# Hybrid decoder layer, one core: the FFN's second weight product by seven block products instead of eight

## The reference

```python
x = layer_norm(ALPHA * x + mix @ w_out, ln1_g, ln1_b)
gate, up = jnp.split(x @ w_ffn_in, 2, axis=-1)             # w_ffn_in: 1024 x 5632
x = layer_norm(ALPHA * x + (jax.nn.silu(gate) * up) @ w_ffn_out, ln2_g, ln2_b)   # w_ffn_out: 2816 x 1024
```

## Time and profile before

| | before |
|---|---|
| time, 3 runs | 2395.21, 2398.1 (median), 2398.82 us |
| span of the profiled execution, first to last instruction | 2396.9 us |
| TensorE busy in it | 2353.9 us (98%) |
| GpSimd, VectorE, ScalarE busy | 1246.0, 1317.3, 1003.4 us |
| mean clock granted to TensorE | 0.993 |
| mean DMA rate | 144 GB/s |
| products of pair 1 and 2 | from about 1266 and 1820 us |
| halves of pair 1 and 2 | from about 1617 and 2173 us |

### The profile page before, as it was taken

One profiled execution on the slowest core, in us unless ns is written; L12 is line 12 of the kernel. 1 busy time (PEld: TensorE's weight loads), 2 busy tenths in 40 slices (PEclk: granted clock), 3 DMA queues, 4 the chain that ended last, 5 costly groups with the idle time before them and its releaser, 6 DMA issues.

```text
span 2396.9 us, 33703 instructions
## 1 busy us (share of the span) xinstructions
PE 2353.9 (98%) x12883; PEld 2259.9 (94%) x12883; DVE 1317.3 (55%) x2034; ACT 1003.4 (42%) x1678; POOL 1246.0 (52%) x679
## 2 busy tenths in 40 slices
PE   8899999999999999999999999999999999999997
PEld 7899999999999989999999999999999999999997
DVE  4455564554666564576365765554064675554165
ACT  4335554554555533355343444333243444333243
POOL 4455545544454445455455555555465555555543
PEclk9999999999999999999999999999999999999999
DMA  6444534434366765554543223226543222226453
GB/s 213 135 113 134 152 98 136 121 102 135 110 181 197 230 220 174 207 198 171 213 153 115 81 77 105 82 87 222 196 159 133 82 77 98 89 76 236 158 190 109
DMA packets 147492, 345.31 MB, mean 144 GB/s; under 512 B 14366, under 2 KB 93302, under 8 KB 145142
## 3 DMA queue, kind: packets, MB, share of 16 engines
q1 hardware_dynamic: 147334, 343.17, 44.3%
HBM read 290.30 MB, written 53.84 MB: 144 GB/s over the span
## 4 chain that ended last, share of the span: by engine, by line
PE 90%; DVE 5%; DMA 2%; issue 1%; ACT 1%; SPq 1%; ACTq 0%; DVEq 0%
PE acc L2193 9%; PE acc L2194 9%; PE acc L2197 9%; PE acc L287 9%; PE acc L289 9%; PE acc L288 8%; PE kd L2193 5%; PE kd L2194 5%; PE kd L2197 5%; PE fb L2193 5%; PE fb L2194 5%; PE fb L2197 5%; DVE total L1191 2%; PE fb L643 1%; PE w L620 1%; PE w L633 1%
## 5 line engine op out<-in xcount | busy, mean ns | idle before, releaser
L262 POOL TENSOR_TENSOR wlo<-raw,whi 128x1024 fp32r<-128x1024 f32 x150 | 371.0, 2476 | 464.9 <-ACT whi L256 464.7
L287 PE MATMUL acc<-xh,whi 128*128 128x416 f32 x1200 | 433.1, 361 | 0.0
L289 PE MATMUL acc<-xh,wlo 128*128 128x416 f32 x1200 | 425.3, 354 | 0.0
L288 PE MATMUL acc<-xl,whi 128*128 128x416 f32 x1200 | 422.4, 352 | 0.0
L1994 POOL TENSOR_TENSOR l_wlo<-l_raw,blocks_hi 128x512 fp32r<-128x512 f32 x176 | 226.6, 1298 | 200.1 <-DVE l_raw L2320 150.7
L256 ACT ACTIVATE whi<-raw 128x1024 fp32r<-128x1024 f32 x150 | 158.6, 1057 | 386.8 <-PE acc L289 264.1
L287 PEld LDWEIGHTS acc<-xh,whi 128*128 128x128 f32 x1200 | 227.7, 190 | 8.5 <-issue 6.3
L1994 POOL TENSOR_TENSOR sums_r<-sums,blocks_hi 128x512 fp32r<-128x512 f32 x132 | 170.6, 1293 | 116.0 <-ACT blocks_hi L2056 89.7
L288 PEld LDWEIGHTS acc<-xl,whi 128*128 128x128 f32 x1200 | 227.7, 190 | 3.0 <-issue 0.2
L289 PEld LDWEIGHTS acc<-xh,wlo 128*128 128x128 f32 x1200 | 227.2, 189 | 2.9
L2193 PE MATMUL acc<-low_r,blocks_hi 128*128 128x416 f32 x608 | 216.9, 357 | 0.0
(11 more groups left out here) (507 smaller groups left out, 5710.7 us busy)
## 6 DMA issues: line engine op xcount, KB each, us to landing
l_raw<-in_wB SPq DMA_DIRECT2D x132, 512.0 KB, 3.5
raw<-in_wA SPq DMA_DIRECT2D x110, 512.0 KB, 3.5
half_R<-in_w SPq DMA_DIRECT2D x52, 704.0 KB, 4.2
raw<-in_wB SPq DMA_DIRECT2D x40, 512.0 KB, 4.5
half_S<-in_w SPq DMA_DIRECT2D x25, 704.0 KB, 4.3
xraw<-in_xT SPq DMA_DIRECT2D x32, 416.0 KB, 5.1
hb<-temps SPq DMA_DIRECT2D x44, 208.0 KB, 1.9
stage<-in_xT SPq DMA_DIRECT2D x40, 208.0 KB, 4.1
```

The costliest lines, as they stand in the source:

```text
L262: self.nc.gpsimd.tensor_tensor(self.wlo[:, n % 4], self.raw[:, n % 4], self.whi[:, n % 3].bitcast(F32), ALU.subtract).then_inc(self.lo_don ...
L287: pe.matmul(bank[:, 0:TG], hi[:, a], self.xh[x][:, a], start=(a == 0), stop=False)
L288: pe.matmul(bank[:, 0:TG], hi[:, a], self.xl[x][:, a], start=False, stop=False)
L289: last = pe.matmul(bank[:, 0:TG], lo[:, a], self.xh[x][:, a], start=False, stop=(a == KD - 1))
```

## The change

For a pair, the second product becomes seven block products too. The output's two 512-feature halves by two token groups are the blocks of the result; the hidden values' two 1408-row halves by two groups are the operands B11 (first half, first group), B12, B21 and B22, with T1 = B12 - B11, T2 = B22 - T1, T3 = B22 - B12, T4 = B21 - T2. `SECOND` gives the order of the seven products; each has 4 steps (`QUARTER`) of 11 tiles: 28 steps (`SECOND_STEPS`, run by `seconds`) in place of 32.

- **Hidden tiles.** The products' `j` now run in the order 0, 11, 1, 12, ... (`TILE_AT`), so that both halves of a tile pair are at hand. `hidden` makes T1 to T4 tile by tile. B11 and T2 stay inside; T1, B21, B22, T3 and T4 are stored (`hid`, `spill`), and loaded again in three pieces (4, 4 and 3 tiles), each rounded by ScalarE (`round_piece`) and split by VectorE (`split_piece`), while the product before runs. TensorE waits for each piece in the first step of a product.
- **Weight sums.** Four sums of w_ffn_out's blocks are made once, in pair 1's products, by GpSimd, in 12 batches (`j` = 1 to 12) of 4, 4 or 3 tiles: load four pieces, four `tensor_tensor`, store four pieces (`w2s`). Both pairs load them as weights.
- **Results.** `take` combines the products on VectorE, one to three operations a step in place of one in two steps. All results of P1 are copied out by ScalarE (`copy_first`).
- **Norms.** The norm of group 0 moves from pair 1's products into its second product (`SECOND_NORM`), that of group 2 has the same places in pair 2's; that of group 3 is at steps 16 to 25 there. The last norm's first mean is taken over six tiles, not seven.

The core of the diff (the moves of code that only change names are left out):

```diff
+SECOND = ("P1", "P6", "P2", "P7", "P4", "P5", "P3")
+QUARTER = KD // 2
+SECOND_STEPS = len(SECOND) * QUARTER
+SPILLED = ("T1", "B21", "B22", "T3", "T4")
+CUTS = ((0, 4), (4, 8), (8, 11))
+    wsum = Store(nc, LOW_AT + 12 * TILE).sb("wsum", [P, 4, 4, P])
+    W_BATCHES = 12
+    def w_batch(j):
+        return j - 1 if 1 <= j <= W_BATCHES else None
...
 sync (SP):
+        def load_weight_pieces(j):
+            jj, k = divmod(w_batch(j), len(CUTS))
+            a, b = CUTS[k]
+            if w_batch(j):
+                sp.wait_ge(w_out, W_OUT + 64 * w_batch(j))
+            for i, n in enumerate((2 * (QUARTER + jj), 2 * (QUARTER + jj) + 1, 2 * jj, 2 * jj + 1)):
+                sp.dma_start(wsum[:, i, 0:b - a], io["w2"][n, :, a:b]).then_inc(w_in, 16)
+        def store_weight_pieces(j):
+            sp.wait_ge(w_made, W_MADE + 4 * (w_batch(j) + 1))
+            for i, s in enumerate((2, 0, 1, 3)):
+                sp.dma_start(io["w2s"][s, jj, :, a:b], wsum[:, i, 0:b - a]).then_inc(w_out, 16)
...
         for r in (1, 2):
             for n, j, name in pair_steps():
                 through(sp, base(r) + n)
...
+                if r == 1 and name == "P6" and j and w_batch(j - 1) is not None:
+                    store_weight_pieces(j - 1)
+                if r == 1 and name == "P7" and w_batch(j) is not None:
+                    load_weight_pieces(j)
...
 gpsimd:
+        def sum_weights(j, name):
+            if name == "P1":
+                pool.wait_ge(w_in, 64 * (n + 1))
+                nc.gpsimd.tensor_tensor(a22, a21, a22, ALU.add).then_inc(w_made, 1)
+                pool.wait_ge(w_made, W_MADE + 4 * n + 1)
+                nc.gpsimd.tensor_tensor(a21, a11, a21, ALU.subtract).then_inc(w_made, 1)
+            if name == "P3":
+                pool.wait_ge(w_made, W_MADE + 4 * n + 2)
+                nc.gpsimd.tensor_tensor(a11, a22, a11, ALU.subtract).then_inc(w_made, 1)
+                pool.wait_ge(w_made, W_MADE + 4 * n + 3)
+                nc.gpsimd.tensor_tensor(a12, a12, a11, ALU.subtract).then_inc(w_made, 1)
...
                 pool.wait_ge(adds, 4 * ((r - 1) * KF + j) + (3 if name == "P1" else 4))
-                rest(weights(r, j, name, True), weights(r, j, name, False), blocks_hi[:, n % 4], base(r) + n)
-            halves(r, 2 * HALVES)
+                rest(weights(j, name, True), weights(j, name, False), blocks_hi[:, n % 4], base(r) + n)
+                if r == 1:
+                    if name == "P1" and j and w_batch(j - 1) is not None:
+                        sum_weights(j - 1, name)
+                    if name == "P3" and w_batch(j) is not None:
+                        sum_weights(j, name)
+            halves(r, SECOND_STEPS)
...
 vector, hidden():
             if name == "P3":
                 signal(nc.vector.tensor_tensor(u4, u4, result("P3"), ALU.add))
                 dve.wait_ge(copies, copied(r, j, "GATE_B"))
-                signal(nc.vector.tensor_tensor(up_b, up_b, u4, ALU.mult))
+                if not odd:
+                    signal(nc.vector.tensor_tensor(b12_tile, up_b, u4, ALU.mult))
+                    dve.wait_ge(combines, combined(r, j, "HB"))
+                    signal(nc.vector.tensor_tensor(t1_tile, b12_tile, u2, ALU.subtract))
+                else:
+                    signal(nc.vector.tensor_tensor(b22_tile, up_b, u4, ALU.mult))
+                    dve.wait_ge(combines, combined(r, j, "HB"))
+                    signal(nc.vector.tensor_tensor(t2, b22_tile, t1_tile, ALU.subtract))
+                    signal(nc.vector.tensor_tensor(b12_tile, b22_tile, b12_tile, ALU.subtract))
+                    dve.wait_ge(combines, combined(r, j, "T2"))
+                    signal(nc.vector.tensor_tensor(t4_tile, b21_tile, t2, ALU.subtract))
...
 vector, take(), of a step whose result is out:
+            if name == "P7":
+                nc.vector.tensor_tensor(c21, c21, out, ALU.add).then_inc(joins, 1)
+                with_residual(c22, out, evac)
+            if name == "P5":
+                nc.vector.tensor_tensor(u, u, out, ALU.add).then_inc(evac, 1)
+                nc.vector.tensor_tensor(c22, c22, u, ALU.add).then_inc(joins, 1)
+                if r == 2:
+                    with_residual(c12, u, joins)
...
 vector, the order in pair 1 and 2:
+        def second_step(r, i):
+            take(r, i)
+            for p, k in pieces_at(r, i):
+                split_piece(r, p, k)
+            for name, part, of in SECOND_NORM.get(i, ()):
+                norm_part(5 if r == 1 else 7, name, part, of)
+            if r == 1:
+                tokens(2, i - X_AT_HALF[2])
+        for i in range(SECOND_STEPS - 1):
+            second_step(2, i)
+            if i == 20:
+                over_some(norm.total[:], third[:, 4:8]).then_inc(parts_done, 1)
+                nc.vector.tensor_tensor(norm.total[:], norm.total[:], first_sum, ALU.add).then_inc(norm.summed, 1)
...
 tensor, seconds():
+                products(bank(i + 2), half_step(r, i), half[b][1][:], half[a][1][:],
+                         [(operand_tile(place, c, 0), operand_tile(place, c, 1)) for c in range(HALF)],
+                         True, True, piece_count(r, p, 0) if p and i % QUARTER == 0 else None)
+                if r == 2 and i == 21:
+                    norm.take_mean(pe, 8)
```

More of the change, by code:

```diff
@@ new lines, in operand_piece, with operand_place @@
+    def operand_piece(place, k, part, rounded=True):
+        a, b = CUTS[k]
+        if place == 0:
+            o = (0, 2 * HALF)[part]
+            return low(o + a, o + b, rounded)
+        if place == 1:
+            o = (2 * HALF, 4 * HALF)[part]
+            return low(o - b, o - a, rounded)
+        o = (0, HALF)[part]
+        return (high_r if rounded else high)[:, o + a:o + b]
+    def operand_place(r, p):
+        return 2 if (r, SECOND[p]) == (2, "P3") else p % 2
+    needs = {"P1": "B11", "P6": "T2", "P2": "B21", "P7": "T3", "P4": "T4", "P5": "T1", "P3": "B22"}
@@ new lines, in kept_outside @@
+    def kept_outside(name, a, b):
+        if needs[SECOND[1]] == name or needs[SECOND[3]] == name or needs[SECOND[5]] == name:
+            a, b = HALF - b, HALF - a
+        return io["hid"][SPILLED.index(name), :, a:b]
+    made = lambda i: low(12 + 5 + i, 13 + 5 + i)[:, 0]
+    t1_tile, b12_tile, t4_tile, b21_tile, b22_tile = (made(i) for i in range(5))
+    wsum = Store(nc, LOW_AT + 12 * TILE).sb("wsum", [P, 4, 4, P])
+    W_BATCHES = 12
+    def w_batch(j):
+        return j - 1 if 1 <= j <= W_BATCHES else None
@@ new lines, in round_tokens, with halves @@
+        def round_tokens(r, i):
+            if not 0 <= i < 7:
+                return
+            b = SPLITS[i]
+            act.wait_ge(t_made, 4 * r)
+            if r == 2 and b in ("T1", "T2", "T3"):
+                act.wait_ge(z_out[("T1", "T2", "T3").index(b)], Z_OUT + 64)
+            nc.scalar.activation(block(HI_AT[b])[1], block(LO_AT[b])[0], ACT.Copy).then_inc(S["x1_hi"], 1)
+        def halves(n):
+            for i in range(n):
+                if i == 1:
+                    round_half(0, 3)
+                if i >= 2 and i + 2 < n:
+                    round_half(0, i + 2)
+                if i == n - 2:
+                    for q in range(4):
+                        round_block(1, q)
+                round_tokens(1, i - X_AT_HALF[1] - 3)
@@ L2120, in halves, with seconds @@
+        def seconds(r, n):
+            for i in range(n):
+                if i < QUARTER:
+                    copy_first(r, i)
                 if i == 1:
@@ L2489, in vector @@
+        dve.wait_ge(S["evac"], evacuated(2, 26))
         dve.wait_ge(norm.mean_full, NORMS + 1)
         move(0, 4)
[L2491 removed]
+        move(4, 6)
+        move(6, 7)
         dve.wait_ge(norm.squared, NORMS + 1)
[L2493 to L2498 removed]
```

707 lines of the change are left out of this document (436 added, 271 removed).

## The result

The changed kernel takes 2452.2 us (median of 4 runs, 2447.8 to 2453.3), the kernel before 2396.8. The ratio is 1.023, with a 95% interval from 1.022 to 1.024: slower, inside the stated range (2375 to 2465), but with +55 us twice what was forecast (+26). The profiled execution has a span of 2450.1 us.

A forecast was written before the change was run, and what follows sets the result against it. It took TensorE, busy nearly throughout, to bound the kernel, so removed steps save time and waits cost it. -49.9 + 57.6 + 8 + 5 + 4 + 1 + 0.5 = +26.2 on 2396.9 gave 2424 us, range 2375 to 2465.

The forecast's parts named there:

- the landing: Pair 1's products: a batch's weight pieces reach SBUF 9.6 us after P6's end, bounds 9.0 and 10.6.
- the wait "at one place": Second product of pair 1: step 20's weights come 4 to 6 us too late behind other DMA traffic.
- What goes, -49.9: Both second products: 32 steps become 28 for a pair, 8 less in all at 6.24 us each, 49.9 us less.
- GpSimd's new work, +57.6: Pair 1's products: GpSimd's sums wait for loads, so TensorE waits 5.4 us a full batch, 3.6 a small; 57.6 more.
- The clock, +8: Behind the batches' waits and later ones: TensorE's clock falls to its lower level, 8 us more, bounds 0 and 22.
- Second product of pair 1, +5: Second product of pair 1: a loaded DMA queue makes step 20's weights late, 5 us more, bounds 0 and 12.
- the rival of VectorE as the bound: Second product: VectorE splits each of the seven operands late, not only at one place; 2450 us, chance 0.12.
- Second product of pair 2, +4: Second product of pair 2: the mean behind step 21 waits 5.2 us for VectorE; net 4 more, bounds 0 and 10.
- Products of pair 2, +1: Pair 2's products: making T1 to T4 adds VectorE operations that delay later work at odd `j`; 1 us more.
- Rival, GpSimd's wait costs little: Pair 1's products: pieces land early enough that the sums cost 0.4 us a batch, 5 in all; 2359 us, chance 0.17.
- Rival, the clock stays down: Pair 1's products: half of the batches' 250 us run at 1.2 GHz, some 40 us more; 2460 us, chance 0.06.

The follow-up runs named there:

- the best version: The changed kernel with weight-sum batches every 12 product steps, one sum behind each GpSimd rest, and gains, token loads, token operations and splits moved: 2350.5 us, ratio 0.981.
- run c: The changed kernel with loads, stores and every wait kept, but each weight sum covering only 8 columns of one tile: 2418.4 us.
- run b: The changed kernel with GpSimd's 48 weight sums made on pieces loaded only once, nothing stored, and four products reading given slabs: 2394.0 us.
- k_no_stores: The changed kernel without the 48 stores of the weight sums; loads wait for the previous batch's sums, four products read given slabs: 2444.1 us.

## Why the prediction was right in kind and short by half

Of the 27 us between the forecast and the measured span, 13.5 lie in the second product of pair 1, 12.1 in pair 1's products and 4.0 in the second product of pair 2; pair 2's products give 3.6 back. So two steps failed, of about the same size: the landing, and the wait "at one place".

- *What goes, -49.9.* Right: 28 steps in each second product, 6.24 to 6.29 apart, and the best version collects nearly all of it.
- *GpSimd's new work, +57.6: the step that failed is the landing, "I take 9.6", with the bound of 10.6.* It was 11.7 in the mean of the full batches. The small ones were 0.6 sooner, as I had it. 0.4 of the error is a later issue; the rest is the time in flight, where I had counted from the fourth issue with "less some for half the bytes": pieces of 256 KB took 4.5 each, slabs of 512 KB 4.8. P5's rest ends 18.8 past P6's end in the batch shown, late by 6.0; over the twelve batches it is late by 72.1 in all (6.6 in a full batch, forecast 5.4, and 4.9 in a small one, forecast 3.6). The VectorE operation between didn't come, VectorE being idle too. The Trainium skill's figure (DMA: Bandwidth & Descriptors, the anatomy of one DMA), by which they would be there at 9.1 (an estimate), was further off from the 10.5 to 12.6 measured.
- *The clock, +8.* The sums cost 79.0 us; the stage grew by 1.3 less, as a norm's two small matmuls left it. Behind the 72.1 of P5's rests 6.9 are left, so the term holds if one counts it as I did. The seen waits (55.3) and the rest divide it otherwise, since half-rate work hides P5's wait; that the two were entangled was foreseen, not its extent. That it comes out near 8 is partly luck: in run c slow work took 15.5 us.
- *Second product of pair 1, +5, a wait "at one place", at most 12.* Failed: it was 18.5, at three places. Step 20 had 3.4. Step 16 had 3.2, from a gain of ScalarE whose place ahead of a rounding I had not looked at, since I had costed ScalarE by its idle share alone. Step 24 had 8.8 (9.2 to the end of its low part). I had written that VectorE has 8 to 11 us of work for 6.24 at steps 16 to 22, and charged nothing for it; this was the rival of VectorE as the bound, and it came true at one operand of six. That this rival's 2450 us lies beside the measured 2452 is chance: nearly half of what was missing came from the landing.
- *Second product of pair 2, +4.* It was 8.0. The wait at the mean was 5.2, as worked out to the tenth, and by the same chain: three operations, the split, the reduction and the sum end 1.9, 6.8, 9.8 and 11.5 behind step 20 (forecast 2.0, 7.0, 10.1, 11.5). The same gain at step 16 (3.2) and slow work behind the waits were missing.
- *Products of pair 2, +1.* They were 2.6 shorter. The steps are 2.31 apart in before and 2.29 in after, without waits in either; why stays open.
- *Rival, GpSimd's wait costs little.* It asked for a landing below 6.5. With the data there the sums still cost 25.2 us (b), not 5; with the waits of the second products that is level with before (ratio 0.9995, 0.998 to 1.001), not faster.
- *Rival, the clock stays down.* It did not: the granted clock is 0.86 to 0.90 in the five windows of 50 us from 1300 to 1550, so with two levels 20 to 28% of that time is at the lower one, not half.

## What to carry to other kernels

Work given to an engine with spare time is costed by what stands behind it in that engine's order, not by its share of idle time: the same 48 sums with their loads cost 79, 6 or 0 us, and without loads 25 or 10, by where they stood and when their data came. Where an engine waits in order for a load, put the load a fixed number of steps ahead, and free the timetable from the loop that happens to be there. When a schedule is shortened, go through every engine's order for each step, since work that had slack beside 32 steps may not have it beside 28; and where an engine is full, as VectorE is at the end, reordering moves a wait and doesn't remove it.

## What the runs showed of the hardware

- TensorE's clock after an idle time: behind waits of 1.44 to 3.00 us the four matmuls took 1.01 to 1.03 us, behind 3.10 to 4.38 they took 1.75 or 1.76 (run c, twelve waits), against 0.93 without a wait. Other runs don't keep to that division: 2.49 was followed by 1.50 and 3.49 by 1.13 (k_no_stores). From 1300 to 1500, windows of 50 us had a clock of 1.00, 1.00, 0.97 and 1.00 in run b, whose waits are 2.0 at most there, and 0.86 to 0.90 in after.
- VectorE's operations hold GpSimd's as well as the other way round: 1.30 us became 1.62 (run b), and a VectorE split of 1.88 became 4.93 between two GpSimd operations, which became 4.83 and 4.91 from 3.2.
- In one stretch of after, loads of 192 KB in a burst of four took 3.8 us each, loads of 256 KB 4.5, and loads of 512 KB 4.8; in the same stretch of before the 512 KB took 3.5. So a load's own bytes don't tell its time; what else is under way counts. Which of the other transfers does it wasn't tried one by one, except the sums' stores (0.6 to 0.7 us of the landing).
